# Experts with 112 seats in the main path instead of 128, overflow in two further rounds of 128

## The chip, the cores and the metric

One core of one Trainium2 chip runs the whole kernel. The time is the device time of one execution in microseconds (us); less is better. In what follows PE is TensorE, PEld its loading of stationary operands, DVE is VectorE, ACT is ScalarE, POOL is GpSimd and SP is SyncE, which issues the weight loads.

## The reference, cut to what matters

A sequence of 256 tokens of width 1024 passes three transformer layers. The change touches only the mixture of experts that ends the second of them:

```python
def moe_swiglu(h, w_router, w_gate_up, w_down):
    ...
    logits = (t @ w_router).astype(F32)
    top_val, top_idx = lax.top_k(logits, TOP_K)            # TOP_K = 2
    top_w = jax.nn.softmax(top_val, axis=-1)
    ...
    for e in range(N_EXPERTS):                              # 8
        gt, up = jnp.split(t @ w_gate_up[e], 2, axis=-1)    # 1024 -> 2 x 3584
        y = (jax.nn.silu(gt) * up) @ w_down[e]              # 3584 -> 1024
        out = out + combine[:, e:e + 1].astype(t.dtype) * y
```

Each token goes to 2 of 8 experts, 512 assignments in all, 64 for an expert on average. How many an expert gets depends on the data, so a kernel with a fixed number of places for an expert needs a way out for a crowded one. With the reference's inputs (seed 0) the eight experts get 55, 74, 53, 86, 71, 54, 55 and 64 tokens.

## The kernel before

All weights are float32 in DRAM. SP loads them in pieces of 512 KB into a ring `raw` of 6 units of 1 MB (128 x 2048). For each unit ACT makes a rounded copy `w_hi` (L1110) and DVE the remainder `w_lo` (L1824), both in the 4-byte type float32r that TensorE multiplies in one pass. A product of weights with activations is then three matmuls of 512 weight columns: w_hi with the high part of the activations (L3060), w_hi with their low part (L3061), w_lo with the high part (L3068). All three lines stand in `consume`, which is called once for a unit: 4 blocks of 512 columns, so 12 matmuls.

In every one of these the weights are the moving operand (512 columns) and the activations the stationary one. In the experts the stationary operand is a block of `slot_hi` or `slot_lo`: 128 values of the model's width (rows) by 128 seats (columns). A seat is a place for one token of the expert; empty seats hold zeros. The bank of results has the seats as partitions.

An expert is 7 steps of 512 hidden columns, a pair of experts 14, all experts 56. In a step TensorE does four units of `up` for the next step's hidden columns (gate and up, banks 0 to 3) and two units of `down` for this step's (banks 4 and 5). Between the first and the second unit of `up` it turns the hidden values, four transposes (L3650, `turn_hidden`): stationary is a 128 x 128 block of `e_hid`, moving is the identity matrix `ident` (a part of the tensor `con`). Around them ACT applies silu (L1529, `e_gated`), DVE multiplies (L2550, `e_hid`), and after the turn ACT takes the high part (L1533, `e_hid_hi`) and DVE the remainder (L2554, `e_hid_lo`); `down` waits for the latter. The order is written out by hand; all engines follow semaphores.

The rows of an expert are gathered from DRAM by POOL (`rows`) and turned into slots (L3684). Its results leave through `y_rows` to `y_dram` (POOL, L1017), from where they are gathered by token at the end. `y_dram` has 256 rows for each expert, as two blocks of 128: one for the main path, one for overflow. The blocks that the main path does not write are zeroed early, by nine DMAs of POOL (L971). The last expert's rows are not stored; they are multiplied straight into the tokens (L3762).

If an expert has more tokens than `capacity`, `flag` is set, and behind the main path each engine branches into a second pass over all experts (`experts(more_ring, more_loop, 1)`), a loop `Fori` over pairs of experts. In the profiled execution this branch is not taken.

Of the kernel before, what the change touches and what calls it, by code (L numbers as in the profile page):

```python
# [47 lines left out]
CAPACITY = 128  # L48
# [113 lines left out]
def program(nc, A, consts, buckets, out, semaphores, numbers, known, stages, capacity):  # L162
# [17 lines left out]
    with ctx:  # L180
# [95 lines left out]
        y_dram = nc.dram_tensor("y_dram", (EXPERTS * 2 * P, D), F32, kind="Internal").ap()  # L276
# [355 lines left out]
        h_again = rows[:, :, :]  # L632

        def y_place(e, again):

            return y_dram.rearrange("(e two p) d -> p e two d", two=2, p=P)[:, bass.ds(e, 1), again, :].rearrange("p e d -> p (e d)")
# [117 lines left out]
        def expert_order(eng, first, pair, again):  # L754

            first()
            if again:
                with eng.Fori(0, EXPERTS // 2 - 1) as d:
                    pair(d, False)
            else:  # L760
                for d in range(EXPERTS // 2 - 1):
                    pair(d, False)
            pair(EXPERTS // 2 - 1, True)
# [5 lines left out]
        def _(sp):  # L769
# [96 lines left out]
            if have("experts"):  # L866
                def experts(R):
# [11 lines left out]
                    def pair(d, last):  # L879
                        for j in range(PAIR_STEPS):  # L880
                            g = FIRST_STEP + RING * j
                            e, step = 2 * d + j // EXPERT_STEPS, j % EXPERT_STEPS
# [3 lines left out]
                            up(g, PAIR_STEPS * d, 2 * d + (j + 1) // EXPERT_STEPS, (j + 1) % EXPERT_STEPS)  # L886
                            down_rows(g + PROLOGUE, PAIR_STEPS * d, e, step)
# [7 lines left out]
                with sp.If(more > 0):  # L895
# [7 lines left out]
                    sp.wait_ge(more_ring.hi, RING + G["in_2"] - G["experts"])  # L903
                    sp.wait_ge(more_ring.lo, RING + G["in_2"] - G["experts"])
# [23 lines left out]
        def _(pool):  # L928
# [37 lines left out]
            if have("experts"):  # L966
# [37 lines left out]
            if have("experts"):  # L1004
# [10 lines left out]
                def store(e):  # L1015
                    pool.wait_ge(L.y_out, e + 2)
                    pool.dma_start(y_place(e, 0), y_rows[:, e % 2, :]).then_inc(L.y_stored, 16)  # L1017
# [11 lines left out]
                pool.wait_ge(y_cleared, 16 * (EXPERTS + 1))  # L1029
# [67 lines left out]
        def _(act):  # L1097
# [419 lines left out]
            if have("experts"):  # L1517
                S.stage("experts")

                def experts(R, L, again):  # L1520
                    def units(g, rounds):

                        return g - R.first + R.credit + 1 + RING * rounds

                    def silu(p, g, rounds, n):
# [3 lines left out]
                        act.activation(e_gated[:, :], bank[2 * p][:, :], ACT.Silu).then_inc(L.gated, 1)  # L1529
# [12 lines left out]
                    def y_leaves(buffer, g, rounds, e):  # L1542
# [3 lines left out]
                        for k in range(2):  # L1546
                            c = act.activation(y_rows[:, buffer, k * 512:(k + 1) * 512], bank[4 + k][:, :], ACT.Copy)
                        c.then_inc(L.y_out, 1)
                        if again:
                            act.wait_ge(L.y_out, e + 2)  # L1550
                            act.dma_start(y_place(e, 1), y_rows[:, buffer, :]).then_inc(L.y_stored, 16)
# [23 lines left out]
                    def pair(d, last):  # L1575
                        r = PAIR_STEPS * d
                        for j in range(PAIR_STEPS):
                            g, n = FIRST_STEP + RING * j, PAIR_STEPS * d + j + 1
                            p, half, step = j % 2, j // EXPERT_STEPS, j % EXPERT_STEPS
                            if last and j == PAIR_STEPS - 1:  # L1580
                                if again:
                                    y_leaves(1, g + 1, r, LAST)
# [18 lines left out]
                            if step == EXPERT_STEPS - 1:  # L1601
                                y_leaves(half, g + 5, r, 2 * d + half)
# [6 lines left out]
                def last_y():  # L1609
                    act.wait_ge(expert_loop.y_free, EXPERTS)  # L1610
                    act.wait_ge(*at("last", "bank", 0))
                    act.activation(y_rows[:, 1, 0:512], bank[4][:, :], ACT.Copy).then_inc(halves[0], 1)
                    act.wait_ge(ring.used, G["in_2"])
                    act.activation(y_rows[:, 1, 512:D], bank[5][:, :], ACT.Copy).then_inc(halves[1], 1)
# [3 lines left out]
                with act.If(more > 0):  # L1618
# [6 lines left out]
                    act.wait_ge(more_ring.used, RING + G["in_2"] - G["experts"])  # L1625
# [184 lines left out]
        def _(dve):  # L1810
# [641 lines left out]
            if have("route"):  # L2452
# [45 lines left out]
                if capacity < P:  # L2498

                    dve.tensor_scalar(pairs_gt[:, 0, 0:2 * EXPERTS], flat(place[:, 0]), capacity - 0.5, 1000.0,  # L2500
                                      ALU.is_gt, ALU.mult).then_inc(S(), 1)
                    dve.wait_ge(*S.last())
                    dve.tensor_tensor(flat(place[:, 0]), flat(place[:, 0]), pairs_gt[:, 0, 0:2 * EXPERTS], ALU.add)\
                       .then_inc(S(), 1)
                    dve.wait_ge(*S.last())

            def route_rest():
# [6 lines left out]
                dve.scalar_tensor_tensor(out=pairs_eq[:, :, 0:EXPERTS], in0=number, scalar=2.0 * P, in1=order,  # L2514
# [6 lines left out]
                if capacity < P:  # L2521

                    dve.tensor_scalar(pairs_eq[:, :, 16:16 + EXPERTS], order, capacity - 0.5, float(P - capacity), ALU.is_gt, ALU.mult)\
                       .then_inc(S(), 1)
                    dve.wait_ge(*S.last())
                    dve.tensor_tensor(pairs_eq[:, :, 0:EXPERTS], pairs_eq[:, :, 0:EXPERTS], pairs_eq[:, :, 16:16 + EXPERTS],
                                      ALU.add).then_inc(S(), 1)
                    dve.wait_ge(*S.last())
# [15 lines left out]
            if have("experts"):  # L2544
                S.stage("experts")

                def experts(R, L, again):
                    def hidden(p, n):
                        dve.wait_ge(L.gated, n)
                        dve.tensor_tensor(e_hid[:, :], e_gated[:, :], bank[2 * p + 1][:, :], ALU.mult).then_inc(L.hidden, 1)  # L2550

                    def hidden_lo(p, n, hi=e_hid_hi, lo=e_hid_lo):
                        dve.wait_ge(L.hid_hi, n)
                        dve.tensor_tensor(flat(lo[:, :, :]), bank[2 * p][:, :], f32(flat(hi[:, :, :])), ALU.subtract)\  # L2554
                           .then_inc(L.hid_lo, 1)
# [11 lines left out]
                    def pick_tokens(e):  # L2567

                        for t in range(TILES):
                            if again:  # L2570
                                o = dve.tensor_scalar(pick[:, t, 0:P], iota, place[:, 1, t, bass.ds(e, 1)], None, ALU.is_equal)
# [104 lines left out]
                with dve.If(more > 0):  # L2676
# [22 lines left out]
                    ordered(dve.tensor_copy(y_row[:, :], flat(row_f[:, :, :])))  # L2699
                    dve.sem_inc(more_ring.lo, RING)  # L2700
                    experts(more_ring, more_loop, 1)
                    dve.wait_ge(more_loop.y_free, EXPERTS + 2)
# [342 lines left out]
        def _(pe):  # L3045
# [592 lines left out]
            if have("experts"):  # L3638
                S.stage("experts")
                def experts(R, L, again):  # L3640
                    def up(p, buffer, h, g, rounds):
                        consume(R, g + h, rounds,
                                [(bank[2 * p + c][:, :], [(slot_hi[:, buffer, 2 * h + k, :], slot_lo[:, buffer, 2 * h + k, :],
                                                           k * 1024 + c * 512, 512) for k in range(2)], h == 0, h == 3)
                                 for c in range(2)])

                    def turn_hidden(p, n):
# [426 lines left out]
```

## Time and profile before

| what | value |
|---|---|
| three runs | 1776.09, 1775.26, 1775.71 us, median 1775.71 |
| span of the profiled execution, first to last instruction | 1773.5 us |
| between its span and the median of the runs | 2.2 us |
| mean granted TensorE clock | 0.998 of full speed |
| expert stage, 496 to 1448 us | 952 us, 54% of the span |
| in it: PE, DVE, ACT busy | 950.4, 845.7, 709.9 us |

The profiled execution has no time listed of its own; its span is 2.2 us under the median of the runs, and that rest lies outside the first and last instruction. A busy time is the sum of an engine's instructions with overlaps counted once; ends of matmuls are modelled, so the pace of a row of matmuls is read from their starts.

### The profile page before, as it was taken

How to read it: one execution, taken by the hardware profiler on the slowest of the kernel's cores; microseconds unless marked ns; L12 is line 12 of the kernel's file. 1: busy time of each engine (PE TensorE's matmuls, PEld its weight loads, DVE VectorE, ACT ScalarE, POOL GpSimd, SP SyncE). 2: the span in 40 equal slices, each digit the busy share in tenths (PEclk: the TensorE clock that was granted, in tenths of full speed). 3: DMA queues.
4: the chain of work that ended last, by engine and by line, in shares of the span. 5: the costliest groups of instructions: out<-in, count | busy, mean ns of one | idle time of the engine just before them, and what ended most of it. 6: DMA issues, size and time to landing. Idle time of an engine off the chain costs nothing.

```text
span 1773.5 us, 22138 instructions
## 1 busy us (share of the span) xinstructions
PE 1744.2 (98%) x8337; PEld 1430.8 (81%) x8346; DVE 1409.3 (79%) x1216; ACT 1115.4 (63%) x1029; POOL 117.5 (7%) x150
## 2 busy tenths in 40 slices
PE   8989999999999999999999999999999999999998
PEld 6778888788778888888888888888888768878886
DVE  5657787867788888888888888888888987576555
ACT  6755444554467777777777777777777766653333
POOL 1111111121020000000000000000002010000000
PEclk9999999999999999999999999999999999999999
DMA  9827999652389999999999999999999996545550
GB/s 327 276 81 269 328 318 331 222 190 94 119 297 375 385 385 378 375 390 381 382 379 379 380 384 377 389 361 383 381 372 386 395 318 203 159 138 187 182 183 25
DMA packets 241627, 525.95 MB, mean 297 GB/s; under 512 B 16858, under 2 KB 48858, under 8 KB 241392
## 3 DMA queue, kind: packets, MB, share of 16 engines
q1 hardware_dynamic: 227856, 477.26, 74.6%
q0 software_dynamic: 13648, 47.29, 7.8%
q8 instruction: 64, 1.05, 0.2%
q14 instruction: 43, 0.35, 0.1%
q10 hardware_dynamic: 16, 0.00, 0.0%
HBM read 513.95 MB, written 10.53 MB: 296 GB/s over the span
## 4 chain that ended last, share of the span: by engine, by line
PE 93%; DVE 4%; ACT 1%; issue 1%; DMA 0%; DVEq 0%; SPq 0%; ACTq 0%
PE bank L3060 26%; PE bank L3068 26%; PE bank L3061 26%; PE bank L3110 2%; PE bank L3119 1%; PE bank L3128 1%; DVE w_lo L1824 1%; PE bank L3650 1%; PE bank L3271 1%; PE bank L3175 1%; ACT w_hi L1110 1%; PE bank L3231 1%; PE bank L3182 0%; PE bank L3212 0%; PE bank L3086 0%
## 5 line engine op out<-in xcount | busy, mean ns | idle before, releaser
L1824 DVE TENSOR_TENSOR w_lo<-raw,w_hi 128x2048 fp32r<-128x2048 f32 x453 | 1040.3, 2299 | 185.8 <-ACT w_hi L1110 174.7
L1110 ACT ACTIVATE w_hi<-raw 128x2048 fp32r<-128x2048 f32 x453 | 867.7, 1916 | 451.6 <-PE bank L3061 304.3
L3060 PE MATMUL bank<-w_hi,slot_hi 128*128 128x512 f32 x896 | 355.2, 396 | 0.0
L3061 PE MATMUL bank<-w_hi,slot_lo 128*128 128x512 f32 x896 | 349.4, 390 | 0.0
L3068 PE MATMUL bank<-w_lo,slot_hi 128*128 128x512 f32 x896 | 240.7, 390 | 1.6 <-DVE w_lo L1824 1.6
L3060 PE MATMUL bank<-w_hi,hT_hi 128*128 128x512 f32 (+1 forms) x568 | 222.7, 393 | 0.1
L3061 PE MATMUL bank<-w_hi,hT_lo 128*128 128x512 f32 (+1 forms) x568 | 219.2, 387 | 0.0
L3068 PEld LDWEIGHTS bank<-w_lo,slot_hi 128*128 128x128 f32 x896 | 167.7, 188 | 39.2 <-DVE w_lo L1824 3.9
L3061 PEld LDWEIGHTS bank<-w_hi,slot_lo 128*128 128x128 f32 x896 | 168.4, 188 | 33.3
L3060 PEld LDWEIGHTS bank<-w_hi,slot_hi 128*128 128x128 f32 x896 | 168.4, 188 | 33.3
L3060 PE MATMUL bank<-w_hi,e_hid_hi 128*128 128x512 f32 x440 | 171.3, 389 | 0.0
L3061 PE MATMUL bank<-w_hi,e_hid_lo 128*128 128x512 f32 x440 | 171.2, 389 | 0.0
L3068 PE MATMUL bank<-w_lo,hT_hi 128*128 128x512 f32 (+1 forms) x568 | 140.4, 389 | 0.0
L3060 PEld LDWEIGHTS bank<-w_hi,hT_hi 128*128 128x128 f32 x568 | 106.7, 188 | 22.1 <-issue 0.6
L3061 PEld LDWEIGHTS bank<-w_hi,hT_lo 128*128 128x128 f32 x568 | 106.8, 188 | 20.7
L3068 PEld LDWEIGHTS bank<-w_lo,hT_hi 128*128 128x128 f32 x568 | 104.6, 188 | 22.4 <-issue 1.7
L3068 PE MATMUL bank<-w_lo,e_hid_hi 128*128 128x512 f32 x440 | 117.6, 389 | 0.0
L3068 PEld LDWEIGHTS bank<-w_lo,e_hid_hi 128*128 128x128 f32 x440 | 82.6, 188 | 17.2
L3061 PEld LDWEIGHTS bank<-w_hi,e_hid_lo 128*128 128x128 f32 x440 | 82.6, 188 | 17.1
L3060 PEld LDWEIGHTS bank<-w_hi,e_hid_hi 128*128 128x128 f32 x440 | 82.6, 188 | 17.1
L3060 PE MATMUL bank<-w_hi,hid_hi 128*128 128x512 f32 x208 | 81.1, 390 | 0.0
L3061 PE MATMUL bank<-w_hi,hid_lo 128*128 128x512 f32 x208 | 81.0, 389 | 0.0
(445 smaller groups left out, 1593.7 us busy)
## 6 DMA issues: line engine op xcount, KB each, us to landing
raw<-in_moe_w_gate_up SPq DMA_DIRECT2D x448, 512.0 KB, 5.8
raw<-in_moe_w_down SPq DMA_DIRECT2D x224, 512.0 KB, 5.9
raw<-in_w_ff SPq DMA_DIRECT2D x64, 512.0 KB, 4.4
work<-in_w_ada POOLq DMA_DIRECT2D x48, 512.0 KB, 5.6
raw<-in_dense_w_gate_up SPq DMA_DIRECT2D x44, 512.0 KB, 5.6
raw<-in_b_w_in SPq DMA_DIRECT2D x24, 512.0 KB, 5.1
raw<-in_w_in SPq DMA_DIRECT2D x24, 512.0 KB, 5.0
raw<-in_dense_w_down SPq DMA_DIRECT2D x22, 512.0 KB, 5.4
```

The lines of the kernel that those rows point to most:

```text
L1110: act.activation(w_hi[:, g % SPLIT, 0:n], raw[:, g % RING, 0:n], ACT.Copy).then_inc(R.hi, 1)
L1824: dve.tensor_tensor(w_lo[:, g % SPLIT, 0:n], raw[:, g % RING, 0:n], f32(w_hi[:, g % SPLIT, 0:n]), ALU.subtract).then_inc(R.lo, 1)
L3060: pe.matmul(out_, hi, w_hi[:, s, c:c + w], start=(start and n == 0), stop=False, skip_group_check=True)
L3061: mm = pe.matmul(out_, lo, w_hi[:, s, c:c + w], start=False, stop=False, skip_group_check=True)
L3068: mm = pe.matmul(out_, hi, w_lo[:, s, c:c + w], start=False, stop=(stop and n == len(terms) - 1), skip_group_check=True)
L3110: pe.matmul(out_, hT_hi[:, k, t * P:(t + 1) * P], w_hi[:, s, c:c + n], start=(start and k == 4 * h), stop=False, skip_group_check=True)
L3119: mm = pe.matmul(out_, hT_lo[:, k, t * P:(t + 1) * P], w_hi[:, s, c:c + n], start=False, stop=False, skip_group_check=True)
L3128: mm = pe.matmul(out_, hT_hi[:, k, t * P:(t + 1) * P], w_lo[:, s, c:c + n], start=False, stop=(not start and k == 4 * h + 3), skip_group_c ...
L3175: mm = pe.transpose(bank[b][:, i * P:(i + 1) * P], src[:, t, k * P:(k + 1) * P], ident)
L3231: mm = pe.matmul(it.values[:, c:c + it.dv], w, v, start=(n == 0), stop=(n == len(terms) - 1))
L3271: mm = pe.matmul(d.level_place(level, n), dk[r, h // d.per, t * P:(t + 1) * P], dq[r, h // d.per, t * width:(t + 1) * width], start=True, ...
L3650: mm = pe.transpose(bank[2 * p][:, k * P:(k + 1) * P], e_hid[:, k * P:(k + 1) * P], ident)
```

## The change

The main path gets 112 seats (`CAPACITY = 112`, `seats_`): the stationary operands of `up` and `down` are cut to 112 columns, banks, `e_gated`, `e_hid` and `y_rows` to 112 partitions, and the turned hidden values lie in 4 x 112 columns instead of 4 x 128. `y_dram` has 256 rows in a run for each expert: 112 from the main path, 128 and 16 from two further rounds, for which the branch now loops over experts instead of pairs. The zeroing is cut anew: rows 112 to 239 of each expert, rows 0 to 111 of the last one, and the 16 ending rows of all in four more DMAs. Gathering and slots still have 128 seats.

```diff
-CAPACITY = 128
+CAPACITY = 112
...
-                for e, again in [(e, 1) for e in range(EXPERTS)] + [(LAST, 0)]:
-                    pool.dma_start(y_place(e, again).rearrange("p (a d) -> p a d", a=4),
-                                   y_zero[:, :].unsqueeze(1).broadcast_to([P, 4, 256])).then_inc(y_cleared, 16)
+                for e, first, n in [(e, capacity, P) for e in range(EXPERTS)] + [(LAST, 0, capacity)]:
+                    pool.dma_start(y_place(e, first, n).rearrange("p (a d) -> p a d", a=4),
+                                   y_zero[0:n, :].unsqueeze(1).broadcast_to([n, 4, 256])).then_inc(y_cleared, 16)
+                ending = P - capacity
+                for a in range(4):
+                    pool.dma_start(y_dram.rearrange("(e q) d -> q e d", q=SEQ)[SEQ - ending:SEQ, :, 256 * a:256 * a + 256],
+                                   y_zero[0:ending, :].unsqueeze(1).broadcast_to([ending, EXPERTS, 256])).then_inc(y_cleared, 16)
...
-                        act.activation(flat(dst[:, :, :]), bank[2 * p][:, :], ACT.Copy).then_inc(L.hid_hi, 1)
+                        n_cols = EHID // P * seats_
+                        act.activation(flat(dst[:, :, :])[:, 0:n_cols], bank[2 * p][:, 0:n_cols], ACT.Copy).then_inc(L.hid_hi, 1)
...
                     def up(p, buffer, h, g, rounds):
                         consume(R, g + h, rounds,
-                                [(bank[2 * p + c][:, :], [(slot_hi[:, buffer, 2 * h + k, :], slot_lo[:, buffer, 2 * h + k, :],
-                                                           k * 1024 + c * 512, 512) for k in range(2)], h == 0, h == 3)
+                                [(bank[2 * p + c][0:seats_, :], [(slot_hi[:, buffer, 2 * h + k, 0:seats_],
+                                                                  slot_lo[:, buffer, 2 * h + k, 0:seats_],
+                                                                  k * 1024 + c * 512, 512) for k in range(2)], h == 0, h == 3)
                                  for c in range(2)])
...
-                            mm = pe.transpose(bank[2 * p][:, k * P:(k + 1) * P], e_hid[:, k * P:(k + 1) * P], ident)
+                            mm = pe.transpose(bank[2 * p][:, k * seats_:(k + 1) * seats_], e_hid[0:seats_, k * P:(k + 1) * P],
+                                              ident[0:seats_, 0:seats_])
...
-                                [(bank[4 + c][:, :], [(hi[:, 2 * h + k, :], lo[:, 2 * h + k, :], k * D + c * 512, 512)
-                                                      for k in range(2)], first and h == 0, last and h == 1) for c in range(2)])
+                                [(bank[4 + c][0:seats_, :], [(hidden_columns(hi, 2 * h + k), hidden_columns(lo, 2 * h + k),
+                                                              k * D + c * 512, 512) for k in range(2)],
+                                  first and h == 0, last and h == 1) for c in range(2)])
```

No instruction changes its place on PE, DVE, ACT or SP; shapes change. On PE, around a turn of hidden values (shapes are of the result, partitions x columns), before:

```order
863 L3061 MATMUL bank<-w_hi,slot_lo 128x512
864 L3068 MATMUL bank<-w_lo,slot_hi 128x512 x4
865 L3650 MATMUL bank<-con,e_hid 128x128 x4
866 L3060 MATMUL bank<-w_hi,slot_hi 128x512
867 L3061 MATMUL bank<-w_hi,slot_lo 128x512
```

And after:

```order
863 L3067 MATMUL bank<-w_hi,slot_lo 112x512
864 L3074 MATMUL bank<-w_lo,slot_hi 112x512 x4
865 L3662 MATMUL bank<-con,e_hid 128x112 x4
866 L3066 MATMUL bank<-w_hi,slot_hi 112x512
867 L3067 MATMUL bank<-w_hi,slot_lo 112x512
```

The weights still stream 512 columns; the turn's moving identity has 112 columns, its stationary block 112 rows by 128 columns. On POOL the zeroing of `y_dram` grows by four DMAs, ahead of the gain multiplications of the first mixer (`mix<-mix,gain`), before:

```order
20 L967 MEMSET y_zero 128x256
21 L971 DMA y_dram<-y_zero 512x1x256 x9
22 L978 ISA
23 L978 TENSOR_TENSOR mix<-mix,gain 128x2x128 x6
24 L717 MEMSET work 128x512
```

And after:

```order
20 L974 MEMSET y_zero 128x256
21 L978 DMA y_dram<-y_zero 512x1x256 x8
22 L978 DMA y_dram<-y_zero 448x1x256
23 L982 DMA y_dram<-y_zero 16x8x256 x4
24 L989 ISA
25 L989 TENSOR_TENSOR mix<-mix,gain 128x2x128 x6
26 L718 MEMSET work 128x512
```

What follows on POOL stands behind 13 DMA issues instead of 9.

## Rows read from the trace of the kernel before

**Rows 1.** The page: span, busy time and share, and GB/s by slice.

```profile
span 1773.5 us, 22138 instructions
PE 1744.2 (98%) x8337; PEld 1430.8 (81%) x8346; DVE 1409.3 (79%) x1216; ACT 1115.4 (63%) x1029; POOL 117.5 (7%) x150
...
GB/s 327 276 81 269 328 318 331 222 190 94 119 297 375 385 385 378 375 390 381 382 379 379 380 384 377 389 361 383 381 372 386 395 318 203 159 138 187 182 183 25
```

**Rows 2.** Windows: us; busy of PE, PEld, DVE, ACT, POOL; PEclk, DMA share, GB/s.

```profile
75.00:88.00 13.00, 13.00 (x72) 10.53 (x71) 10.05 (x32) 8.92 (x23) 0.11 (x1) 1.00 1.01 377
...
496.00:1448.00 952.00, 950.42 (x4336) 784.99 (x4336) 845.65 (x490) 709.91 (x477) 32.37 (x25) 1.00 1.02 379
```

**Rows 3.** Waits of PE in the expert stage: us, times, longest.

```profile
PE bank L3068 <- DVE w_lo L1824: 1.6, 5, 0.8
```

**Rows 4.** PE's timeline in one unit of up: start, us, instruction.

```profile
907.24 0.39 PE L3060 MATMUL bank<-w_hi,slot_hi 128*128 128x512 f32 x1
...
909.96 0.39 PE L3060 MATMUL bank<-w_hi,e_hid_hi 128*128 128x512 f32 x1
```

**Rows 5.** Expert stage, groups by line and shape: count, busy us, mean ns.

```profile
L3068 PE MATMUL bank<-w_lo,slot_hi 128*128 128x512 f32 x896 | 240.7, 390 | 1.6 <-DVE w_lo L1824 1.6
L3061 PEld LDWEIGHTS bank<-w_hi,slot_lo 128*128 128x128 f32 x896 | 168.4, 188 | 33.3
L3068 PE MATMUL bank<-w_lo,e_hid_hi 128*128 128x512 f32 x440 | 117.6, 389 | 0.0
L2554 DVE TENSOR_TENSOR e_hid_lo<-bank,e_hid_hi 128x512 fp32r<-128x512 f32 x55 | 37.6, 683 | 0.0
L3650 PE MATMUL bank<-con,e_hid 128*128 128x128 f32 x224 | 33.5, 271 | 0.0
L1533 ACT ACTIVATE e_hid_hi<-bank 128x512 fp32r<-128x512 f32 x55 | 31.9, 579 | 0.0
L3650 PEld LDWEIGHTS bank<-con,e_hid 128*128 128x128 f32 x224 | 27.8, 139 | 7.2
```

**Rows 6.** Whole span, loads of narrower or shorter stationary blocks.

```profile
L3523 PEld LDWEIGHTS bank<-work,one_row 128*32 128x32 f32 x24 | 0.6, 108 | 1.3 <-issue 1.3
L3625 PEld LDWEIGHTS bank<-con,plain 8*128 8x128 f32 x2 | 0.2, 135 | 1.1 <-DVE plain L2463 1.1
```

**Rows 7.** PE's timeline elsewhere; the last row: durations of one, min/median/max.

```profile
378.19 0.28 PE L3060 MATMUL bank<-w_hi,hT_hi 128*128 128x256 f32 x1
...
379.63 1.12 PE L3068 MATMUL bank<-w_lo,hT_hi 128*128 128x256 f32 x8
...
489.39 1.89 PE L3182 MATMUL bank<-con,zero 128*128 128x512 bf16 x8 [0.16 <-issue]
...
L3182 PE MATMUL bank<-con,zero x76: 377/379/634, 121.4 to 1581.6; 128*128 128x512 bf16 x76
```

**Rows 8.** PE's timeline: float32 rows of 128 and of 64 moving columns.

```profile
390.23 2.84 PE L3271 MATMUL bank<-work 128*128 128x128 f32 x24
...
406.57 2.79 PE L3271 MATMUL bank<-mix,proj 128*128 128x64 f32 x24
```

**Rows 9.** PE's timeline around a turn of hidden values.

```profile
918.12 0.60 PE L3650 MATMUL bank<-con,e_hid 128*128 128x128 f32 x4
918.48 0.48 PE L3060 MATMUL bank<-w_hi,slot_hi 128*128 128x512 f32 x1
918.79 0.40 PE L3061 MATMUL bank<-w_hi,slot_lo 128*128 128x512 f32 x1
...
921.34 1.03 PE L3684 MATMUL bank<-con,rows 128*128 128x128 f32 x8
```

**Rows 10.** POOL's timeline behind the zeroing, and SP's waits from 60 to 100 us.

```profile
66.98 6.66 POOL L971 DMA_DIRECT2D y_dram<-y_zero  x9 [29.83 <-ACT proj L1341]
87.89 0.73 POOL L978 TENSOR_TENSOR mix<-mix,gain 128x256 f32<-128x256 f32 x1 [14.26 <-DVE headsq L1947]
...
SPq L776 <- DVE w_lo L1824: 32.7, 6, 7.7
```

More of the change, by code:

```diff
@@ L632, in program, with y_place @@
         h_again = rows[:, :, :]
-        def y_place(e, again):
-            return y_dram.rearrange("(e two p) d -> p e two d", two=2, p=P)[:, bass.ds(e, 1), again, :].rearrange("p e d -> p (e d)")
+        again_place = pairs_gt[:, :, 32:32 + 2 * EXPERTS]
+        def y_place(e, first, n):
+            return y_dram.rearrange("(e q) d -> q e d", q=SEQ)[first:first + n, bass.ds(e, 1), :].rearrange("p e d -> p (e d)")
         def gla_rankT():
@@ L757, in expert_order @@
             if again:
-                with eng.Fori(0, EXPERTS // 2 - 1) as d:
+                with eng.Fori(0, EXPERTS - 1) as d:
                     pair(d, False)
+                pair(EXPERTS - 1, True)
             else:
@@ L879, in pair, with expert @@
                     def pair(d, last):
+                        def expert(j):
+                            n = j // EXPERT_STEPS
+                            return (2 * d + n) // 2 if R is more_ring else 2 * d + n
                         for j in range(PAIR_STEPS):
                             g = FIRST_STEP + RING * j
-                            e, step = 2 * d + j // EXPERT_STEPS, j % EXPERT_STEPS
+                            e, step = expert(j), j % EXPERT_STEPS
                             if last and j == PAIR_STEPS - 1:
@@ L1540, in slots, with y_leaves @@
                         c.then_inc(L.slots_hi, 1)
-                    def y_leaves(buffer, g, rounds, e):
+                    def y_leaves(buffer, g, rounds, e, expert=None):
                         act.wait_ge(R.used, units(g, rounds))
@@ L1546, in y_leaves @@
                         for k in range(2):
-                            c = act.activation(y_rows[:, buffer, k * 512:(k + 1) * 512], bank[4 + k][:, :], ACT.Copy)
+                            c = act.activation(y_rows[0:seats_, buffer, k * 512:(k + 1) * 512], bank[4 + k][0:seats_, :], ACT.Copy)
                         c.then_inc(L.y_out, 1)
@@ L1550, in y_leaves @@
                             act.wait_ge(L.y_out, e + 2)
-                            act.dma_start(y_place(e, 1), y_rows[:, buffer, :]).then_inc(L.y_stored, 16)
+                            first_, rows_ = ((capacity, P), (capacity + P, P - capacity))[buffer]
+                            act.dma_start(y_place(expert, first_, rows_), y_rows[0:rows_, buffer, :]).then_inc(L.y_stored, 16)
                             act.wait_ge(L.y_stored, 16 * e + 16)
@@ L1624, in _ @@
                     experts(more_ring, more_loop, 1)
[L1625 removed]
+                    act.wait_ge(more_ring.used, RING + 2 * (G["in_2"] - G["experts"]))
                 with act.Else():
@@ L2513, in route_rest @@
                 number = con[:, C_IOTA:C_IOTA + EXPERTS].unsqueeze(1).broadcast_to([P, TILES, EXPERTS])
-                dve.scalar_tensor_tensor(out=pairs_eq[:, :, 0:EXPERTS], in0=number, scalar=2.0 * P, in1=order,
+                dve.scalar_tensor_tensor(out=pairs_eq[:, :, 0:EXPERTS], in0=number, scalar=float(SEQ), in1=order,
                                          op0=ALU.mult, op1=ALU.add)
@@ L2547, in experts @@
                 def experts(R, L, again):
+                    seats_ = P if again else capacity
                     def hidden(p, n):
                         dve.wait_ge(L.gated, n)
-                        dve.tensor_tensor(e_hid[:, :], e_gated[:, :], bank[2 * p + 1][:, :], ALU.mult).then_inc(L.hidden, 1)
+                        dve.tensor_tensor(e_hid[0:seats_, :], e_gated[0:seats_, :], bank[2 * p + 1][0:seats_, :], ALU.mult)\
+                           .then_inc(L.hidden, 1)
                     def hidden_lo(p, n, hi=e_hid_hi, lo=e_hid_lo):
                         dve.wait_ge(L.hid_hi, n)
-                        dve.tensor_tensor(flat(lo[:, :, :]), bank[2 * p][:, :], f32(flat(hi[:, :, :])), ALU.subtract)\
-                           .then_inc(L.hid_lo, 1)
+                        n_cols = EHID // P * seats_
+                        dve.tensor_tensor(flat(lo[:, :, :])[:, 0:n_cols], bank[2 * p][:, 0:n_cols], f32(flat(hi[:, :, :])[:, 0:n_cols]),
+                                          ALU.subtract).then_inc(L.hid_lo, 1)
                     def slots(buffer, n):
@@ L2699, in _ @@
                     ordered(dve.tensor_copy(y_row[:, :], flat(row_f[:, :, :])))
+                    for n in range(2):
+                        ordered(dve.tensor_scalar(again_place.rearrange("p t (e r) -> p t e r", r=2)[:, :, :, n], place[:, 1],
+                                                  -float(n * P), None, ALU.add))
                     dve.sem_inc(more_ring.lo, RING)
                     experts(more_ring, more_loop, 1)
-                    dve.wait_ge(more_loop.y_free, EXPERTS + 2)
+                    dve.wait_ge(more_loop.y_free, 2 * EXPERTS + 2)
                     dve.sem_inc(again_run, 1)
@@ L3761, in _ @@
                     pe.wait_ge(*at("last", "y", c))
-                    pe.matmul(bank[LAST_BANKS[c, t]][:, :], last_turned[t], y_rows[:, 1, c * 512:(c + 1) * 512], start=True, stop=True)\
+                    pe.matmul(bank[LAST_BANKS[c, t]][:, :], last_turned[t][0:capacity, :], y_rows[0:capacity, 1, c * 512:(c + 1) * 512],
+                              start=True, stop=True)\
                       .then_inc(S("last", "product", c, t), 1)
```

49 lines of the change are left out of this document (20 added, 29 removed).

## The prediction

> **What bounds the kernel now.** I read the page first. TensorE is busy for 1744 of 1773.5 us, and no other engine comes near it [rows 1]. By stage the experts take 952 us, and in them TensorE is busy for 950.4; DVE follows with 846 and ACT with 710 [rows 2]. The waits say the same from the other side: in that stage TensorE was held up by another engine for 1.6 us in all, five times, each time by DVE's `w_lo` [rows 3]. So the stage is as long as its row of matmuls, and a change is worth what it does to their pace or their number. The DMAs run at 379 GB/s with their share at 1.02 [rows 2]: they keep up, but have little to spare; the fastest slice of the page has 395 [rows 1].
>
> The pace comes from the timeline. One unit is 12 matmuls of 512 moving columns and takes 909.96 - 907.24 = 2.72 us, 226.7 ns for one [rows 4]. The stage has 3 x 896 of them in `up`, 3 x 440 in `down` [rows 5] and 24 more in its last step, together 56 steps x 72 = 4032; at 226.7 ns they make 914 of the 952 us. The rest is mostly turning: four transposes in each step.
>
> **The big matmuls.** They keep their 512 moving columns; what shrinks is the stationary block, 128 columns to 112. A load of 128 columns shows 188 ns [rows 5], one of 32 columns 108 [rows 6]: (188 - 108)/96 = 0.83 ns for a column, so 16 columns fewer are 13.3 ns less of load. But the load is not what ends last: it takes 188 of the 226.7 ns, and the loads of that group sit idle for 33.3 us over 896, 37 ns each [rows 5]. What makes the pace otherwise? 256 moving columns go at about 120 ns: (379.63 - 378.19)/12 [rows 7]. From 256 to 512 it grows by 106.7 ns, 0.417 for a column, which is one column per cycle of the full 2.4 GHz clock (granted 1.00 in the stage [rows 2]); so 512 columns are 213 ns of streaming, and 13 ns are a fixed part that is the same for both lengths. A bf16 matmul of 512 columns, also with 128 stationary columns, goes at (1.89 - 0.38)/7 = 216 ns [rows 7], so it pays some 3. The 4-byte matmuls pay about 10.8 ns more, and no row shows whether this hangs on the number of stationary columns, for every such matmul in this kernel has 128. I take nothing for it, because the load has room and the fixed part doesn't follow the one length that does vary. The ends: if the whole 10.8 ns go, 4032 x 10.8 = 44 us less; if the pace gets worse, the nearest row is the one behind a turn, where eleven intervals from 918.79 to 921.34 make 231.8 ns [rows 9], 5.1 more: 4032 x 5.1 = 21 us more.
>
> **The turns.** 224 transposes [rows 5]. Their moving operand goes from 128 to 112 columns, their stationary one from 128 to 112 rows, with 128 columns as before. One takes (0.60 - 0.27)/3 = 0.11 us [rows 5, 9], some 108 ns. If streaming sets that, 16 of 128 columns save 13.5 ns each: 224 x 13.5 = 3.0 us. If loading sets it, nothing comes of it, for the load stays at 128 columns: a transpose with a stationary block of only 8 rows loads in 135 ns, one with 128 rows in 139 [rows 5, 6]. Which of the two it is, two float32 groups tell: 24 with 128 moving columns take 2.84 us, 24 with 64 take 2.79 [rows 8]. Half the columns to stream and the same pace: the load sets it. I take that, and only the block loaded behind the last transpose of a step, which belongs to the next `up` and has 112 columns now, comes 13.3 ns sooner: 56 x 13.3 = 0.7 us. The Trainium skill (TensorE: Matmul & The Clock Gate, LDWEIGHTS) says that a load's time goes by its columns and not by its rows, and gives P/1.2 ns; the trace's 0.83 ns for a column and its 135 against 139 agree, and by that rule, too, the turns give 0.7 and not 3.0.
>
> **ACT and DVE.** `e_hid_hi` and `e_hid_lo` go from 512 to 448 columns. In proportion that is at most 579/8 = 72 ns on ACT and 683/8 = 85 ns on DVE in each of 56 steps [rows 5], 4.1 and 4.8 us. `e_gated`, `e_hid` and `y_rows` keep their columns and lose partitions, which I take to cost nothing. All of it lies beside matmuls: `down` comes three units of `up` behind the turn, some 8 us, and both copies together take 1.3. What it could give back is the 1.6 us for which TensorE waited for DVE [rows 3]; I take 0 and keep 1.6 as a bound.
>
> **POOL and DMA.** Zeroing gets four more issues, at 6.66/9 = 0.74 us each 3 us more on POOL [rows 10]. Behind them stands the first gain multiplication, for which POOL waits 14.26 us anyway [rows 10], so it isn't late. Written are four times 128 KB more and 64 KB less, 0.46 MB, at 377 GB/s 1.2 us of transfer while the DMAs are full (share 1.01 from 75 to 88 us) [rows 2]. The weight loads share those engines, but there SP waits for DVE to empty the ring, 32.7 us in all [rows 10], and TensorE is busy for 13.00 of 13.00 us [rows 2]; without that cover it would be 1.2 us, and I take 0. Stores of results shrink by an eighth, off the path. The new loop in the branch costs nothing where the branch isn't taken.
>
> **The sum.** 1773.5 - 0.7 = 1772.8 us of span, with the same 2.2 us around it 1775.0, against a median of 1775.7. About 0.2% (3.6 us) is what a measurement of this kernel can tell from no change, so this is no change. Its own range, with the bounds of the small terms (3.0 instead of 0.7 for the turns, 1.6 from DVE, 1.2 for the DMAs and some tenths of scatter): 1770.8 to 1777.
>
> **The rivals.**
>
> *The fixed part shrinks with the stationary columns.* A constant that the bf16 row doesn't have and that doesn't depend on the moving length could be a piece of the load that isn't hidden. If it goes in proportion, 10.8 x 16/128 = 1.35 ns x 4032 = 5.4 us, and with the turns 0.7: 1769.6. For it speaks that the 4-byte matmuls alone pay; against it that the load shows 37 ns of room.
>
> *The load is what sets the fixed part.* If 13.3 ns less of load come through whole until the bf16 pace is reached, 44 us go. Then a unit would want its 1 MB sooner, 379 x 226.7/215.9 = 398 GB/s, and the fastest slice has 395 [rows 1]: 952 x (1 - 379/395) = 38.6 us is about what the loads allow, 1737 us. The same page of the Trainium skill (Back-to-back issue gap) says that in a stream of loads and matmuls the spacing is set by both; that is this case, while the 131 ns that it gives for 512 columns are far from the 226.7 here.
>
> *The pace falls apart: slower.* Behind the turn shown, eleven intervals average 231.8 ns, while a unit that no turn disturbs goes at 226.7 [rows 4, 9]; so the steady pace may be one that load and matmul have to find with each other. A load of another length might not find it. From half of the matmuls at 231.8 the kernel is slower by 10 us, with all of them by 21: 1796 us. Against it: loads of 128 columns settle everywhere in this trace, with 256 moving columns too.
>
> *An expert with over 112 tokens*, and two further rounds of 8 experts would come, at 952 us for each round: some 3700 us. The reference's inputs give at most 86, so only other inputs could do it.
>
> **Chances.** No change to the pace, 60%, of which 4 points fall below -0.2% by the small terms; in proportion 17%; the whole fixed part 13%; slower pace 8%; other, overflow included, 2%. Faster by over 0.2%: 17 + 13 + 4 = 34%; within: 56%; slower: 10%. The range leaves out the whole fixed part, the overflow and the upper half of the slower pace, 19%: 1767 to 1786 us.
>
> **What would show it.** Right: a unit of 12 matmuls still takes 2.72 us, loads of 112 columns show about 175 ns with 50 ns of room, the turns' pace stays at 108 ns, `e_hid_hi` near 510 to 530 ns, and the zeroing ends 3 us later with the first gain multiplication at the same time. Wrong: another pace of the units in steady state, above all with the same matmuls elsewhere in the kernel unchanged; TensorE waiting for `w_hi` or `w_lo` in the experts; or a second round in the trace.

## The result, and the profile after

The changed kernel takes 1781.24 us (median of 6 runs, 1780.18 to 1782.95), the kernel before 1775.97 (6 runs, 1775.26 to 1777.17). The ratio is 1.0031, 95% interval 1.002 to 1.0041: slower by some 5 us, where 1775.0 and no change were forecast. The time lies inside the stated range of 1767 to 1786 us, on the side that was given 10%. The profiled execution took 1782.0 us, 2.0 of them around its span.

The page of the changed kernel, span and busy times, as in [rows 1]:

```profile
span 1780.0 us, 22151 instructions
PE 1751.7 (98%) x8346; PEld 1374.4 (77%) x8346; DVE 1406.2 (79%) x1216; ACT 1112.6 (63%) x1029; POOL 118.8 (7%) x154
```

The same two windows as in [rows 2], with the same columns (us; busy of PE, PEld, DVE, ACT, POOL; granted clock, DMA share, GB/s):

```profile
75.00:88.00 13.00, 13.00 (x72) 10.27 (x72) 9.08 (x28) 7.30 (x20) 1.46 (x2) 1.00 1.03 313
...
496.00:1448.00 952.00, 951.21 (x4306) 723.91 (x4305) 836.00 (x487) 704.89 (x476) 31.61 (x25) 1.00 1.01 375
```

The second window tells the story: TensorE is as busy as before at the same granted clock, yet does 4306 matmuls in the 952 us instead of 4336. Weight loads, DVE and ACT all have less to do. TensorE's wait for another engine in the stage, one row as in [rows 3], has shrunk too:

```profile
PE bank L3074 <- DVE w_lo L1839: 0.6, 1, 0.6
```

So it is not held up; it is slower at what it does, and only at the matmuls that changed: those of `w_hi` and `w_lo` with `hT` and with `hid` in the other stages, also 512 moving columns but untouched, average 227.8 and 227.0 ns from start to start in both traces (intervals under 245 ns). The groups of the stage, as in [rows 5] (count, then busy us and mean ns of one, then idle us ahead of them):

```profile
L3067 PEld LDWEIGHTS bank<-w_hi,slot_lo 128*112 128x112 f32 x896 | 156.3, 174 | 46.1
...
L2557 DVE TENSOR_TENSOR e_hid_lo<-bank,e_hid_hi 128x448 fp32r<-128x448 f32 x55 | 34.1, 619 | 0.0
L3662 PE MATMUL bank<-con,e_hid 112*128 112x112 f32 x224 | 30.6, 258 | 0.0
L1547 ACT ACTIVATE e_hid_hi<-bank 128x448 fp32r<-128x448 f32 x55 | 28.8, 523 | 0.0
L3662 PEld LDWEIGHTS bank<-con,e_hid 112*128 112x128 f32 x224 | 26.4, 140 | 8.4
```

A load takes 174 ns instead of 188, and the idle time before one is 46.1/896 = 51 ns instead of 37: more room than before. TensorE's timeline (start, us, instruction) shows the pace, with the first matmul of five units of 12 in a row, two of `up`, two of `down`, and one of `up` again:

```profile
907.03 0.39 PE L3066 MATMUL bank<-w_hi,slot_hi 128*112 128x512 f32 x1
...
909.78 0.39 PE L3066 MATMUL bank<-w_hi,slot_hi 128*112 128x512 f32 x1
...
912.53 0.39 PE L3066 MATMUL bank<-w_hi,e_hid_hi 128*112 128x512 f32 x1
...
915.30 0.39 PE L3066 MATMUL bank<-w_hi,e_hid_hi 128*112 128x512 f32 x1
...
918.08 0.39 PE L3066 MATMUL bank<-w_hi,slot_hi 128*112 128x512 f32 x1
```

`up` takes 2.75 us for 12, 229 ns each, and `down` 5.55/24 = 231 ns, where both had 2.72 us and 226.7 ns [rows 4].

The whole stage can be added up from the starts of consecutive matmuls in the two traces, from the first matmul of `up` to the last of `down` (without the 24 of the very last step, which read another tensor):

| intervals | count | before, us | after, us | difference |
|---|---|---|---|---|
| `up` to `up` (with the one behind each turn) | 2569 | 593.5 | 596.1 | +2.6 |
| `down` to `down` | 1264 | 286.6 | 292.4 | +5.8 |
| transpose to transpose in a turn | 168 | 18.2 | 16.1 | -2.1 |
| all others | 302 | 47.3 | 47.7 | +0.3 |
| sum | 4303 | 945.7 | 952.4 | +6.6 |

The spans differ by 1780.0 - 1773.5 = 6.5 us. So all of it lies in the big matmuls, and the larger part in `down`, which has a third of them: 231.3 ns for an interval instead of 226.8. In `up` two things are mixed: the first interval behind a turn went from 315.9 to 301.7 ns (55 times, -0.8 us), the others gave +3.4. So the slower pace costs 3.4 + 5.8 = 9.2 us, and shorter turns and what follows them give 2.9 back.

### The profile page after: what moved, and what is told of

Its sections match the earlier page's. It is cut to its first block, busy times and chain, and to the rows that moved or that the text cites. A ratio compares the mean times of both kernels' runs of the same rounds, so it can differ in the third digit from the quotient of the medians.

```text
span 1780.0 us, 22151 instructions
## 1 busy us (share of the span) xinstructions
PE 1751.7 (98%) x8346; PEld 1374.4 (77%) x8346; DVE 1406.2 (79%) x1216; ACT 1112.6 (63%) x1029; POOL 118.8 (7%) x154
## 4 chain that ended last, share of the span: by engine, by line
PE 95%; DVE 3%; ACT 1%; issue 1%; DMA 0%; DVEq 0%; ACTq 0%; SPq 0%
PE bank L3066 27%; PE bank L3074 27%; PE bank L3067 27%; PE bank L3116 2%; PE bank L3125 1%; PE bank L3134 1%; PE bank L3662 1%; PE bank L3277 1%; PE bank L3181 1%; PE bank L3188 1%; DVE w_lo L1839 1%; PE bank L3237 1%; ACT w_hi L1121 0%; PE bank L3218 0%; PE bank L3092 0%
## 5 line engine op out<-in xcount | busy, mean ns | idle before, releaser
L3066 PE MATMUL bank<-w_hi,slot_hi 128*112 128x512 f32 x896 | 356.0, 397 | 0.0
L3067 PE MATMUL bank<-w_hi,slot_lo 128*112 128x512 f32 x896 | 350.8, 392 | 0.0
L3074 PE MATMUL bank<-w_lo,slot_hi 128*112 128x512 f32 x896 | 242.4, 392 | 0.8 <-DVE w_lo L1839 0.6
L3074 PEld LDWEIGHTS bank<-w_lo,slot_hi 128*112 128x112 f32 x896 | 155.7, 174 | 52.1 <-DVE w_lo L1839 3.3
L3067 PEld LDWEIGHTS bank<-w_hi,slot_lo 128*112 128x112 f32 x896 | 156.3, 174 | 46.1
L3066 PEld LDWEIGHTS bank<-w_hi,slot_hi 128*112 128x112 f32 x896 | 156.3, 174 | 45.8
L3066 PE MATMUL bank<-w_hi,e_hid_hi 128*112 128x512 f32 x440 | 172.9, 393 | 0.0
L3067 PE MATMUL bank<-w_hi,e_hid_lo 128*112 128x512 f32 x440 | 172.5, 392 | 0.0
L3074 PE MATMUL bank<-w_lo,e_hid_hi 128*112 128x512 f32 x440 | 120.5, 396 | 0.0
L3066 PEld LDWEIGHTS bank<-w_hi,e_hid_hi 128*112 128x112 f32 x440 | 76.8, 174 | 25.0
```

What stands on the lines that cost most here:

```text
L3066: pe.matmul(out_, hi, w_hi[:, s, c:c + w], start=(start and n == 0), stop=False, skip_group_check=True)
L3067: mm = pe.matmul(out_, lo, w_hi[:, s, c:c + w], start=False, stop=False, skip_group_check=True)
L3074: mm = pe.matmul(out_, hi, w_lo[:, s, c:c + w], start=False, stop=(stop and n == len(terms) - 1), skip_group_check=True)
```

## The experiments

Two things changed for those matmuls. The stationary block has 112 columns instead of 128; and in `down` the four blocks of a step lie 112 x 4 = 448 bytes apart instead of 512, because the turned values are now packed. In `up` the blocks stay 512 bytes apart. Ratios below are to the kernel before on the same chip, with the 95% interval. "Pace" is the mean of all intervals under 245 ns between two matmuls of `up`, or of `down`, which leaves out the first behind a turn; before it is 227.6 and 226.7. The edits are shown cut to what matters: wherever `down` does not read as in the changed kernel, ACT and DVE also copy all 512 turned columns again, and the last step of `down` follows the same edit.

**All 128 columns again, 512 bytes apart; only the turn keeps 112.**

```diff
-   (bank[2 * p + c][0:seats_, :], [(slot_hi[:, buffer, 2 * h + k, 0:seats_], ...
+   (bank[2 * p + c][:, :], [(slot_hi[:, buffer, 2 * h + k, :], ...
-   return flat(buf[:, :, :])[:, k * seats_:(k + 1) * seats_]
+   return flat(buf[:, :, :])[:, k * P:(k + 1) * P]
-   pe.transpose(bank[2 * p][:, k * seats_:(k + 1) * seats_], ...
+   pe.transpose(bank[2 * p][:, k * P:k * P + seats_], ...
```

> All matmuls of up and down get stationary blocks of 128 columns again, 512 bytes apart (the 16 seats too many are computed and not used); only the turn keeps 112 rows and 112 moving columns. If the number of stationary columns makes the pace (theory A), units go back to 226.7 ns a matmul and the turns keep their 96 ns: 168 x 12 ns = 2.1 us, perhaps 0.7 more behind the turn, below the kernel before: 1773 to 1774 us. If something else of the change costs the time (theory B: 112 partitions in ACT and DVE, the turn itself, the zeroing, DMAs), it stays near 1781.

1772.96 us, before 1774.18; ratio 0.999 (0.9981 to 0.9999). Its timeline:

```profile
906.48 0.39 PE L3066 MATMUL bank<-w_hi,slot_hi 128*128 128x512 f32 x1
...
909.20 0.39 PE L3066 MATMUL bank<-w_hi,e_hid_hi 128*128 128x512 f32 x1
...
911.92 0.39 PE L3066 MATMUL bank<-w_hi,e_hid_hi 128*128 128x512 f32 x1
...
914.64 0.39 PE L3066 MATMUL bank<-w_hi,slot_hi 128*128 128x512 f32 x1
```

Units are back at 2.72 us. Paces: 227.4 and 226.7 ns. The turn keeps its 96.1 ns for a transpose. Whatever costs the time is in the blocks, in their count or their places, which this run restores together; and the turn is a gain of its own. The first interval behind a turn is back at 315.4 ns, so its 14 ns did come from the shorter load.

**112 columns, blocks 512 bytes apart in `down` too.**

```diff
-   return flat(buf[:, :, :])[:, k * seats_:(k + 1) * seats_]
+   return flat(buf[:, :, :])[:, k * P:k * P + seats_]
-   pe.transpose(bank[2 * p][:, k * seats_:(k + 1) * seats_], ...
+   pe.transpose(bank[2 * p][:, k * P:k * P + seats_], ...
```

> 112 stationary columns everywhere, but the turned hidden values lie 512 bytes apart for each block instead of 448. If the start of a block within its partition is what makes down slower than up (231.2 against 229.3 ns in the changed kernel), down falls to up's 229.3 and the kernel gains 1320 x 2 = 2.6 us on the changed one: about 1778.5. If the number of columns alone makes both, down stays at 231 and the time at 1781.

1778.85 us, before 1774.18; 1.0025 (1.0015 to 1.0036). The timeline:

```profile
908.20 0.39 PE L3066 MATMUL bank<-w_hi,slot_hi 128*112 128x512 f32 x1
...
910.95 0.39 PE L3066 MATMUL bank<-w_hi,e_hid_hi 128*112 128x512 f32 x1
...
913.69 0.39 PE L3066 MATMUL bank<-w_hi,e_hid_hi 128*112 128x512 f32 x1
...
916.44 0.39 PE L3066 MATMUL bank<-w_hi,slot_hi 128*112 128x512 f32 x1
```

`down` now takes 2.745 us for a unit, as `up` does: paces 229.0 (`down`) and 229.2 ns (`up`). So the distance of 448 bytes cost `down` some 2 ns, and 112 columns cost both some 2 ns over the pace of before.

The first two steps of the stage ran otherwise in this kernel, with the same operands at the same places:

```profile
519.21 0.39 PE L3066 MATMUL bank<-w_hi,e_hid_hi 128*112 128x512 f32 x1
...
522.01 0.39 PE L3066 MATMUL bank<-w_hi,e_hid_hi 128*112 128x512 f32 x1
...
527.34 1.18 PE L3074 MATMUL bank<-w_lo,slot_hi 128*112 128x512 f32 x4 [0.51 <-DVE w_lo L1839]
```

A unit took 2.80 us there (233 ns), and from the third step on, behind a wait of 0.51 us, it took 2.745. So one set of operands can run at two paces, and the stream kept each of them for steps on end.

**128 columns in `down`, starting 448 bytes apart (`up` with 112).** The other half of the pair: the place without the count.

```diff
-   return flat(buf[:, :, :])[:, k * seats_:(k + 1) * seats_]
+   return flat(buf[:, :, :])[:, k * seats_:k * seats_ + P]
-   (bank[4 + c][0:seats_, :], ...
+   (bank[4 + c][:, :], ...
```

> up as in the changed kernel (112 columns), down with 128 stationary columns that begin 448 bytes apart (the last 16 of each overlap the next block, their results are not used). If the count alone sets the pace, down goes back to 226.7 ns: 1320 x 4.5 = 6 us less than the changed kernel, 1775. If the start alone sets what down has beyond up, down comes to about 229 and the time to 1778. If both act together only with 112 columns, anything between.

1781.47 us; 1.0047 (1.0031 to 1.0062). None of the values expected for `down` came:

```profile
912.69 0.40 PE L3066 MATMUL bank<-w_hi,e_hid_hi 128*128 128x512 f32 x1
...
915.46 0.40 PE L3066 MATMUL bank<-w_hi,e_hid_hi 128*128 128x512 f32 x1
...
918.23 0.39 PE L3066 MATMUL bank<-w_hi,slot_hi 128*112 128x512 f32 x1
```

2.77 us for a unit, pace 231.0 ns. With all 128 columns `down` is as slow as in the changed kernel. The place alone costs everything there; the two costs do not add.

**96 seats.** Edit: `CAPACITY = 96` in the changed kernel, so 96 columns, blocks of `down` 384 bytes apart.

> The changed kernel with 96 seats. If the pace worsens as the block gets shorter (theory A, monotonic), up goes above 229.3, say 231.5, and the time to 1787 or more. If it hangs on whether a block ends on a boundary (96 columns are 384 bytes, three quarters of 512), up may settle again at 226.7 or below, and with turns of 82 ns (168 x 26 = 4.4 us less than before) the kernel comes out near 1771.

1781.6 us; 1.0039 (1.0024 to 1.0055). Neither expectation fits: the pace does not settle, and it gets hardly worse (230.0 and 231.4 ns). The loads are down to 162 ns with 57.5/896 = 64 ns of room, and a transpose takes 82.8 ns, which gives back 4.3 us. The groups of the stage:

```profile
L3067 PEld LDWEIGHTS bank<-w_hi,slot_lo 128*96 128x96 f32 x896 | 144.7, 162 | 57.5
...
L3662 PE MATMUL bank<-con,e_hid 96*128 96x96 f32 x224 | 27.7, 245 | 0.0
```

So neither "fewer columns, worse pace" nor "more room, better pace" holds.

**Six other counts and six other distances in one kernel.** Each expert of the kernel before gets its own count of stationary columns in `up` and its own distance between blocks in `down`, there with 128 columns; the turn is as wide as the distance.

```diff
+   COUNT, APART = (128, 124, 120, 116, 104, 96, 80, 128), (128, 126, 124, 120, 96, 64, 104, 128)
-   (bank[2 * p + c][:, :], [(slot_hi[:, buffer, 2 * h + k, :], ...
+   (bank[2 * p + c][0:m, :], [(slot_hi[:, buffer, 2 * h + k, 0:m], ...
-   (bank[4 + c][:, :], [(hi[:, 2 * h + k, :], ...
+   (bank[4 + c][:, :], [(block(hi, 2 * h + k, n), ...
+   return flat(buf[:, :, :])[:, k * apart_of(n):k * apart_of(n) + P]
```

> The kernel before with another number of stationary columns in up for each expert (128, 124, 120, 116, 104, 96, 80, 128) and another distance of the 128-column blocks of down (512, 504, 496, 480, 384, 256, 416, 512 bytes); experts have no more tokens than seats, so results stay right. If only the full 128 columns settle, up shows 226.7 in the first and last expert and 229 to 231 in all others, whatever the number; if the pace grows as the block shrinks, 124 columns stand near 227 and 80 near 232. If starts at other than multiples of 512 bytes cost, down shows about 231 everywhere but in the first and last expert; if multiples of 128 or 256 bytes are enough, the experts at 384 and 256 bytes stay at 226.7.

**Seven more counts, and blocks that start elsewhere.** The same kernel with other numbers; `FROM` moves all blocks of an expert by so many words of 4 bytes.

```diff
+   COUNT, APART = (64, 126, 56, 122, 108, 100, 88, 128), (64, 112, 64, 88, 80, 64, 64, 128)
+   FROM = (32, 0, 16, 0, 0, 8, 64, 0)
```

> The kernel before, by expert: stationary columns of up 64, 126, 56, 122, 108, 100, 88, 128; blocks of 128 columns in down 256, 448, 256, 352, 320, 256, 256 and 512 bytes apart, in the experts 0, 2, 5 and 6 all moved by 128, 64, 32 and 256 bytes. If a steady 226.7 ns needs every block to start at a multiple of 256 bytes (the sweep before: 512 and 256 settle, seven others don't), down settles in the experts 6 and 7 alone and 0, 2 and 5 go to 230 or more; if equal distances are enough, 0, 2 and 5 settle too. For up, where blocks start at multiples of 512 bytes, 64 columns should settle if the length must be a multiple of 256 bytes, and all other numbers but 128 stay between 228 and 233.

Each of the two ran once (1786.0 and 1790.64 us, against 1775.23 and 1775.84 before); what counts is the pace within each expert, in ns. The mean of 128 columns in `up`, 227.6 to 227.7, holds the slower intervals behind a turn; between turns it is 226.7. 112 columns have 229.3 in the changed kernel.

| `up`: columns | 128 | 126 | 124 | 122 | 120 | 116 | 108 | 104 |
|---|---|---|---|---|---|---|---|---|
| pace | 227.6 | 233.2 | 228.1 | 231.1 | 233.2 | 233.3 | 230.3 | 229.3 |

| `up`: columns | 100 | 96 | 88 | 80 | 64 | 56 |
|---|---|---|---|---|---|---|
| pace | 232.7 | 230.0 | 228.9 | 233.1 | 230.1 | 229.3 |

| `down`: distance, bytes | 512 | 504 | 496 | 480 | 448 | 416 | 384 | 352 | 320 | 256 |
|---|---|---|---|---|---|---|---|---|---|---|
| pace | 226.7 | 231.9 | 230.1 | 232.8 | 231.0 | 232.2 | 233.0 | 231.2 | 231.9 | 226.8 |

| `down`, 256 apart, all moved by, bytes | 32 | 64 | 128 | 256 |
|---|---|---|---|---|
| pace | 233.4 | 233.3 | 232.9 | 226.7 |

Two units of `down` of the second kernel, one of the expert moved by 32 bytes and one of that moved by 256:

```profile
1194.48 0.40 PE L3060 MATMUL bank<-w_hi,e_hid_hi 128*128 128x512 f32 x1
...
1197.28 0.40 PE L3060 MATMUL bank<-w_hi,e_hid_hi 128*128 128x512 f32 x1
...
1298.12 0.39 PE L3060 MATMUL bank<-w_hi,e_hid_hi 128*128 128x512 f32 x1
...
1300.84 0.39 PE L3060 MATMUL bank<-w_hi,e_hid_hi 128*128 128x512 f32 x1
```

2.80 us against 2.72, with the same 128 columns, the same distance and the same loads. `down` settles only where its blocks start at multiples of 256 bytes from where they stood before. `up`, which starts there always, settles with 128 columns. The means of the other counts don't tell all, for two of them hide two paces. With 124 columns six of 28 units ran at 226.7 ns and most others at 228.3. With 88 columns the units of the first two steps took 2.80 us; from the third step on they took 2.72, those right behind a turn or the gathered rows aside:

```profile
1243.71 0.40 PE L3060 MATMUL bank<-w_hi,slot_hi 128*88 128x512 f32 x1
...
1246.51 0.39 PE L3060 MATMUL bank<-w_hi,e_hid_hi 128*128 128x512 f32 x1
...
1258.01 0.39 PE L3060 MATMUL bank<-w_hi,slot_hi 128*88 128x512 f32 x1
...
1260.73 0.39 PE L3060 MATMUL bank<-w_hi,slot_hi 128*88 128x512 f32 x1
```

Operands, places and loads (154 ns) are the same in both. What differs is what ran before: the slow ones came behind units of `down` at 2.80 us (the expert moved by 32 bytes), and between the two rows stand the first units of `down` at 2.72 (the expert moved by 256). So fewer columns do not shut out the good pace. The one other count that ran beside a `down` that settles, 96 in the first sweep, stayed at 229.9; the rest ran beside a `down` that does not settle, and what they would do beside one that does is not shown. That holds for 64 columns too, 256 bytes of them, which were expected to settle and did not. Blocks of 128 columns do not depend on this: in the first sweep the last expert's `up` was at 226.6 ns in its first unit, right behind a `down` at 232.

**The weights' side moved.** In `up` of the kernel before, with 128 columns at their old place, the moving operand starts so many words later in each expert. The last of a unit's four blocks has nowhere to go and stays, so three of four are moved.

```diff
+   SHIFT = (0, 4, 8, 16, 32, 64, 96, 0)
-   k * 1024 + c * 512, 512)
+   min(k * 1024 + c * 512 + shift, 1536), 512)
```

> The kernel before with all stationary blocks of 128 columns; in up the moving weights are read from 0, 16, 32, 64, 128, 256, 384 and 0 bytes further on (the last block of a unit as far as it goes), so the experts 1 to 6 multiply by the wrong weight columns. If the stationary block's place and length alone make the pace, all experts show up at 226.7 ns in steady state. If it is how the two reads lie to each other, the experts 1 to 4 and 6 go to 229 or more.

The kernel ran once: 1782.03 us, before 1775.84. Paces of `up` for starts moved by 0, 16, 32, 64, 128, 256, 384 and 0 bytes: 227.7, 231.5, 231.9, 231.5, 232.0, 227.6, 232.0 and 227.7 ns. A unit moved by 32 bytes, and one moved by 256 up to the turn behind it:

```profile
807.10 0.39 PE L3060 MATMUL bank<-w_hi,slot_hi 128*128 128x512 f32 x1
...
809.88 0.39 PE L3060 MATMUL bank<-w_hi,e_hid_hi 128*128 128x512 f32 x1
...
1174.49 0.39 PE L3060 MATMUL bank<-w_hi,slot_hi 128*128 128x512 f32 x1
...
1177.21 0.60 PE L3653 MATMUL bank<-con,e_hid 128*128 128x128 f32 x4
```

2.78 against 2.72 us. It is not a property of the stationary read alone: the moving read loses its pace by some 4 ns when it leaves its place, and has it back 256 bytes further on. The units of `down`, untouched here, felt it too: behind a moved `up` the first of a pair mostly took 228.5 to 230.5 ns a matmul, the second 226.6 again.

**What the experiments point to: full blocks, and 96 columns in the turn alone.** Edit: the first experiment with `CAPACITY = 96`.

> The kernel with 128 stationary columns in up and down and a short turn, now with 96 seats instead of 112 in the turn. If the turn's pace is set by its moving columns (96.1 ns at 112, 82.8 at 96) and the matmuls keep 226.7 ns, the turns give 168 x (108.4 - 82.8) = 4.3 us against the kernel before: about 1770, ratio 0.9976. If the 4-byte load sets the turn's pace below 112 columns, it stays at the 1773 of the run with 112.

1770.89 us, before 1775.23; ratio 0.9975 (0.9966 to 0.9985). The timeline around a turn, and the window of the stage:

```profile
908.18 0.39 PE L3066 MATMUL bank<-w_hi,e_hid_hi 128*128 128x512 f32 x1
...
910.90 0.39 PE L3066 MATMUL bank<-w_hi,e_hid_hi 128*128 128x512 f32 x1
...
916.34 0.49 PE L3662 MATMUL bank<-con,e_hid 96*128 96x96 f32 x4
916.62 0.48 PE L3066 MATMUL bank<-w_hi,slot_hi 128*128 128x512 f32 x1
```

```profile
496.00:1448.00 952.00, 949.49 (x4346) 782.25 (x4346) 846.62 (x492) 712.94 (x483) 30.75 (x25) 1.00 1.02 379
```

4346 matmuls in the 952 us, the most of all, with units at 2.72 us. Transpose to transpose is 82.8 ns, 13.9 us in the stage against 18.2 before: -4.3 us, as much as the whole gain.

## Why the prediction was wrong

**The big matmuls: the step that failed.** The prediction took nothing for them, "because the load has room and the fixed part doesn't follow the one length that does vary". Both observations were right, and neither was a reason for the pace to stay. The load got shorter as worked out (16 columns, 188 to 174 ns, where 13.3 ns were forecast) and its room grew, and the pace got worse by 3.4 us in `up` and 5.8 in `down`: a term put at nothing measured 9.2 us. What sets the pace was not known, and "has room" was read as "has no influence". That the time lies in the stated range all the same is luck: the range reached that far for a rival given 8%, and the turns gave more than was forecast.

**The half that was not seen.** The packing of the turned values was treated as something that shortens two copies. It also moved three of four blocks of `down` off their places. The run with 128 columns 448 bytes apart shows that this alone brings the pace of `down` to 231. Of the +5.8 us, 2.9 go when the blocks lie 512 bytes apart again (292.4 to 289.5 us), the rest with the 128 columns.

**The rival that came, and its mechanism.** "The pace falls apart: slower", at 8%, had the sign, and its nearest row, 231.8 ns behind a turn [rows 9], is close to what `down` now does all the time. Its price of 21 us was for all 4032 at 5.1 ns; measured are 1.7 ns in `up` and 4.5 in `down`. Its mechanism, a load of another length that does not find its pace, is half of the matter. That load and matmul have to find the pace fits the two stretches above, where the same operands ran at two paces. But loads of 128 columns lose it too when they, or the moving operand, start elsewhere. "Against it: loads of 128 columns settle everywhere in this trace" spoke of blocks of 128 columns at places where they settle; no row had a cut or a moved one.

**The two gaining rivals.** Both took the fixed part for a piece of the load. With 96 and fewer columns the load was 26 ns and more shorter than with 128, and the pace never fell below 226.7. They are out.

**The turn: the second step that failed, in the other direction.** "Half the columns to stream and the same pace: the load sets it" was read from two groups [rows 8] whose operations are not the turn's: their loads take 192 ns, the turn's 139 [rows 5]. The loads of the first of the two (shortest, median, longest in ns):

```profile
L3271 PEld LDWEIGHTS bank<-work x24: 190/192/192, 390.1 to 392.7; 128*128 128x128 f32 x24
```

The prediction's own rows spoke against it: loads of 139 ns [rows 5] came every 108 ns, so a load's duration is no floor for the spacing of loads. The turn goes with its moving columns: 108.4, 96.1 and 82.8 ns for 128, 112 and 96, some 0.8 ns a column. (Its stationary rows shrink with them, which no run separates; the load stays at 139 to 140 ns in [rows 5] and after.) The two sweeps, whose turns are as wide as the distance, show where this ends: 69.7 ns with 80 columns, but 78 to 79 with 64. The Trainium skill (TensorE: Matmul & The Clock Gate, LDWEIGHTS) says that a load's time goes by its columns; the loads of the turn agree, 128 columns and no change, but this didn't set the turn's time. The 0.7 us for the block loaded behind the turn were right: 0.8 us, gone again with 128 columns. Together 2.9 us, by chance close to the upper bound of 3.0: that counted 224 transposes, while 168 intervals got shorter (2.1 us) and the 0.8 came on top.

**What was right.** `e_hid_hi` 523 ns, in the forecast 510 to 530, and hidden, as is `e_hid_lo` (619). On POOL, the four further issues took 3.06 us, but began before the ninth ended: zeroing took 8.74 us from first to last instead of 6.66, 2.1 more where 3 were forecast. The first gain multiplication waited 12.17 us instead of 14.26 and was on time. POOL's timeline of the changed kernel, as in [rows 10]:

```profile
65.19 6.63 POOL L978 DMA_DIRECT2D y_dram<-y_zero  x9 [29.85 <-ACT proj L1352]
70.87 3.06 POOL L982 DMA_DIRECT2D y_dram<-y_zero  x4
...
86.10 0.73 POOL L989 TENSOR_TENSOR mix<-mix,gain 128x256 f32<-128x256 f32 x1 [12.17 <-DVE headsq L1962]
```

The DMAs moved 313 instead of 377 GB/s in the 13 us from 75 to 88, and TensorE was busy for all of them: the cover held. No second round ran.

## What to carry to other kernels

When a stream is bound by matmuls, "fewer columns" and "packed closer" are not free even where loads have room: ask whether the operands still start where they did, and keep full blocks of 128 columns at their old places though fewer seats are needed; here that was the one form that always came back to the good pace. Cut instead what the pace does follow, here the moving columns of the transposes, which gave 4.3 us with the big matmuls left as they were. And before a term is set to nothing, ask whether any row of the trace has ever varied what the change varies; if none has, the bound on the bad side deserves more than a few points.

## What the runs showed of the hardware

4-byte matmuls of 512 moving columns settle at 226.7 ns with 128 stationary columns and both reads at multiples of 256 bytes from the places of the kernel before. With another start of either read they averaged 230.1 to 233.4 ns in an expert. With another count at the good places they averaged 228.1 to 233.3; but 88 columns ran at 233.5 ns behind units that did not settle and at 226.7 behind units that did, and 112 columns at 233 and at 229 within one kernel. So count and place do not fix the pace alone, and what ran before has a part in it. The load's length does not order these numbers (181 ns of load and 233.2 with 120 columns, 168 and 229.3 with 104).

Since the start of the moving read matters as much as that of the stationary one, it looks like two reads that get in each other's way, but that is argued and not shown: no run moved both by the same distance, which would tell a bad place from a bad pair of places. Open is also how the count acts, through the load or through the partitions of the result, which change with it; no run here separates these. And no run has an `up` of 112 columns beside a `down` that settles, which would show what 112 columns cost by themselves.
